# A two-block network on one core: when and behind what the first expert's weights are loaded

## The reference

```python
def first_block(x, ...):
    x = x + _mixer(x, ...)                 # three branches a, b, c; merged @ w_out
    x = x + _expert_choice_ffn(x, ...)

def _expert_choice_ffn(x, norm_g, w_router, w_e_gate, w_e_up, w_e_down):
    xn = _rmsnorm(x, norm_g)
    aff = softmax(xn @ w_router)           # 256 tokens x 16 experts
    gate, idx = top_k(aff transposed, 32)  # each expert takes 32 tokens
    xg = xn[idx]
    h = silu(xg @ w_e_gate[e]) * (xg @ w_e_up[e])     # 1024 -> 1536
    yo = (h @ w_e_down[e]) * gate
    return scatter_add(yo, idx)
```

## Time and profile before

| | us |
|---|---|
| median of three runs | 1536.87 (1536.32 to 1538.96) |
| the profiled execution | 1535.79 |
| its span, first to last instruction | 1534.0 |
| TensorE products busy in the span | 1382.4 (90%) |
| VectorE / ScalarE / GpSimd busy | 523.4 / 480.9 / 197.9 |
| bytes moved | 446.84 MB, mean 291 GB/s |

### The profile page before, as it was taken

One profiled execution on the slowest core, in us unless ns is written; L12 is line 12 of the kernel. 1 busy time (PEld: TensorE's weight loads), 2 busy tenths in 40 slices (PEclk: granted clock), 3 DMA queues, 4 the chain that ended last, 5 costly groups with the idle time before them and its releaser, 6 DMA issues. The chain is left out here.

```text
span 1534.0 us, 18841 instructions
## 1 busy us (share of the span) xinstructions
PE 1382.4 (90%) x7568; PEld 903.0 (59%) x7568; DVE 523.4 (34%) x899; ACT 480.9 (31%) x739; POOL 197.9 (13%) x128
## 2 busy tenths in 40 slices
PE   8999999998777888777788887999999999899998
PEld 7888888543322333223223332878888778788886
DVE  5997877300000000000000001735333526653334
ACT  6766653300000000000000001635444457554443
POOL 0020000000000000000000000352222182122221
PEclk9999999999898888888978889999999999999999
DMA  7664448999999999999999999836565454265640
GB/s 252 195 175 124 119 154 328 418 431 430 429 432 431 432 435 431 431 431 429 432 431 432 434 431 418 325 120 210 174 202 184 157 196 137 92 211 173 202 158 28
DMA packets 117938, 446.84 MB, mean 291 GB/s; under 512 B 8568, under 2 KB 61176, under 8 KB 98816
## 3 DMA queue, kind: packets, MB, share of 16 engines
q1 hardware_dynamic: 117312, 445.47, 75.2%
q10 hardware_dynamic: 576, 0.71, 0.2%
HBM read 445.10 MB, written 1.05 MB: 291 GB/s over the span
## 5 line engine op out<-in xcount | busy, mean ns | idle before, releaser
L1488 PE MATMUL ps<-sb_ring,sb_consts 128*32 128x384 f32 x1760 | 191.5, 593 | 85.7 <-DMA sb_ring<-w_e_up 48.6
L170 PE MATMUL ps<-net_whi,sb_xhi 128*128 128x512 f32 x480 | 189.8, 395 | 1.5 <-DVE sb_xlo L2465 1.0
L1488 PEld LDWEIGHTS ps<-sb_ring,sb_consts 128*32 128x32 f32 x1760 | 61.5, 129 | 215.8 <-issue 106.9
L172 PE MATMUL ps<-net_whi,sb_xlo 128*128 128x512 f32 x480 | 187.1, 390 | 0.0
L171 PE MATMUL ps<-net_wlo,sb_xhi 128*128 128x512 f32 x480 | 187.0, 390 | 0.0
L1510 PE MATMUL ps<-sb_e_ring,sb_hT 128*32 128x512 f32 x540 | 178.4, 646 | 3.3 <-DMA sb_e_ring<-w_e_down 3.3
L1980 ACT ACTIVATE net_whi<-sb_ring 128x2048 fp32r<-128x2048 f32 x64 | 122.2, 1918 | 58.4 <-PE ps L172 55.4
L1583 DVE TENSOR_TENSOR sb_sg<-ps,sb_sg 128x384 f32<-128x384 f32 x16 | 8.9, 557 | 363.7 <-PE ps L1488 363.7
L1993 DVE TENSOR_TENSOR net_wlo<-sb_ring,net_whi 128x2048 fp32r<-128x2048 f32 x46 | 107.1, 2332 | 58.2 <-ACT net_whi L1980 58.2
L1993 POOL TENSOR_TENSOR net_wlo<-sb_ring,net_whi 128x2048 fp32r<-128x2048 f32 x18 | 83.7, 4648 | 215.7 <-ACT net_whi L1980 215.7
L1510 PE MATMUL ps<-sb_mid,sb_hT 128*32 128x512 f32 x180 | 105.9, 751 | 5.3 <-DMA sb_e_ring<-w_e_down 5.3
(11 more groups left out here) (369 smaller groups left out, 2056.0 us busy)
## 6 DMA issues: line engine op xcount, KB each, us to landing
sb_ring<-w_e_gate SPq DMA_DIRECT2D x28, 3072.0 KB, 39.1
sb_e_ring<-w_e_down SPq DMA_DIRECT2D x46, 1536.0 KB, 35.1
sb_ring<-ffn_w_gu SPq DMA_DIRECT2D x88, 512.0 KB, 4.6
sb_ring<-w_e_up SPq DMA_DIRECT2D x14, 3072.0 KB, 39.2
sb_ring<-w_e_up SPq DMA_DIRECT2D x20, 1536.0 KB, 40.8
sb_mid<-w_e_up SPq DMA_DIRECT2D x16, 1536.0 KB, 42.0
sb_mid<-w_e_down SPq DMA_DIRECT2D x15, 1536.0 KB, 32.2
sb_ring<-ffn_w_down SPq DMA_DIRECT2D x22, 1024.0 KB, 4.9
```

The source lines that it names most:

```text
L170: pe.matmul(out, hi, whi, start=start, stop=False)
L172: return pe.matmul(out, lo, whi, start=False, stop=stop)
L1488: mm = pe.matmul(ps[j * CAP:(j + 1) * CAP, GATE if i < 4 else UP, 0:FJ], xgs[:, k, :], rows[:, q * E_FF + j * FJ:q * E_FF + (j + 1) * FJ], ...
```

## The change

Five edits in four places. (1) Units 0 to 3 of expert 0 are issued behind granules 69, 72, 75 and 78 in place of one behind granule 80 and three behind 81; the three waits stand ahead of unit 0 as before. (2) Groups 1 to 3 of expert 0 and the pair of expert 1 move from the experts' SyncE program, behind the barrier, into the mixer's, behind a wait for the mixer's last product. (3) The table's load stays where it is, and is now the first that the experts' program issues. (4) `m.spare` and `m.e_ring` are allocated ahead of the mixer, and the mixer's halves `whi`, `wlo`, `xhi`, `xlo` and `yahi` are given addresses under them, so that both can be named at the same time. (5) `WARM` is 3 in place of 4.

```diff
         st = Stream(ctx, nc, "mix", ring[:, :, :], 5, 5, GRAN)
-        st.place_halves(ctx, nc, "mix")
+        st.hi, st.lo, xhi, xlo = m.mix_whi, m.mix_wlo, m.mix_xhi, m.mix_xlo
...
-        xhi, xlo = sb("xhi", [P, DC, SEQ], F32R), sb("xlo", [P, DC, SEQ], F32R)
...
-        yhi = {"a": sb("yahi", [P, 4, SEQ], F32R), "b": xhi[:, 4:DC, :], "c": chi}
+        yhi = {"a": m.mix_yahi, "b": xhi[:, 4:DC, :], "c": chi}
...
+        EARLY_AT = [n_gran - 13, n_gran - 10, n_gran - 7, n_gran - 4]
...
-                if g == n_gran - 2:
-                    sp.wait_ge(yalo, A_HEADS)
-                    sp.wait_ge(yclo, C_HEADS // 2)
-                    sp.wait_ge(conv_step, 4 * B_TAPS)
-                    load_expert(sp, m, I, 0, 0)
-            for i in range(1, EARLY):
+                if g in EARLY_AT:
+                    if g == EARLY_AT[0]:
+                        sp.wait_ge(yalo, A_HEADS)
+                        sp.wait_ge(yclo, C_HEADS // 2)
+                        sp.wait_ge(conv_step, 4 * B_TAPS)
+                    load_expert(sp, m, I, 0, EARLY_AT.index(g))
+            for i in range(RING, EARLY):
                 if i == RING:
                     sp.wait_ge(yblo, 4)
                 elif i == RING + 1:
...
             load_group(sp, m, I, 0, 0)
-
+            sp.wait_ge(st.used, n_gran)
+            for j in range(1, P // CAP):
+                load_group(sp, m, I, 0, j)
+            load_pair(sp, m, I, 1, 0, True)
...
-WARM = 4
+WARM = 3
...
-            load_group(sp, m, I, 0, 1)
             sp.dma_start(late[:, :], I["c_late"][:, 3 * P:]).then_inc(late_in, 16)
-            for j in range(2, J):
-                load_group(sp, m, I, 0, j)
-            load_pair(sp, m, I, 1, 0, True)
             sp.sem_clear(m.mixer_sems)
...
-                mixer(nc, m, I)
+                with ExitStack() as under:
+                    def below(name, shape, side):
+                        return under.enter_context(nc.sbuf_tensor("mix_" + name, [P, *shape], F32R, side=side))
+
+                    m.mix_whi, m.mix_yahi = below("whi", [5, GRAN], "left"), below("yahi", [4, SEQ], "left")
+                    m.mix_wlo = below("wlo", [5, GRAN], "right")
+                    m.mix_xhi, m.mix_xlo = below("xhi", [DC, SEQ], "right"), below("xlo", [DC, SEQ], "right")
                 m.spare = first.enter_context(nc.sbuf_tensor("sb_spare", [P, SPARES * SLOT], F32))
                 m.e_ring = room("e_ring", (SPARE - RING - RING2 - MID) * SLOT)
+                mixer(nc, m, I)
```

## The result

| | before | after |
|---|---|---|
| median, us | 1536.59 (1536.09 to 1538.96, 4 runs) | 1548.51 (1546.58 to 1549.33, 4 runs) |
| ratio to before | | 1.0069, 95% interval 1.0057 to 1.0081 |
| profiled execution, us (span) | 1535.79 (1534.0) | 1546.58 (1544.8) |

The change made the kernel slower by 0.69% (the quotient of the two medians alone would be 1.0078, inside the interval). 1545.5 was forecast, with a range of 1540.2 to 1548.7: the median lies 3.0 us above the forecast and 0.2 us under the range's upper end. The medians lie 11.9 us apart, the profiled executions 10.8. Where the time went shows in the same views as before. The page first: span, and GB/s by slice.

What follows compares the result with a forecast made beforehand. TensorE was taken to bound the mixer and second block, weight transfers the experts. Late table, slow gather, three units and a landing put the first released load at 314.3 against 305.7: +8.6, so 1545.5 us, range 1540.2 to 1548.7.

Steps and rivals of the forecast that it cites:

- The rule: Experts, bound by weight transfers: they move by as much as the landing at 305.7 us of expert 0's first released load.
- The sum: From the table's landing at 294.05 us to the first released load's landing: 314.3 against 305.7, so +8.6 us.
- What is moved past what: SyncE queue: the table's load keeps its order behind groups and pair, lands at 294.05; the rank copy begins 5.9 us later.
- rival A: Load queue: the table overtakes the pair and isn't held back; 1.85 us faster, 1535.0, no measurable change; chance 10%.
- Terms of the sum: Hand-over to expert 0: table 294.05, copy to gather 0.72, gather 7.4, scaling and start 0.6, three units 5.5, landing 6.05.
- Rival B: Gather: the table is late but the clock holds, gather in 3.7 us; +4.9, 1541.8 us; chance 27%.
- The bound of +2.2: Expert 0's hidden products: at most 2.2 us more if all three units run at the lower clock.
- I cost this at nothing in the mixer: Mixer: gate unit loads among the granules delay nothing; were the cover gone, at most 4 x 3.7 us.
- the loads have cover: Mixer: loads are issued six granules ahead, so a granule landing up to 3.7 us later holds nothing up.
- The idle product, hidden by the wait: Before the turn of the ranks: one product fewer saves 0.9 us, worth nothing while the table is late.
- Rival A's price: Table early: 0.95 us less queueing plus 0.9 us for the idle product, 1.85 us faster, 1535.0.

Runs made afterwards that it cites:

- table-first kernel: The changed kernel with the table's load issued behind group 0, ahead of the wait for the mixer's last product: 1539.27 us, ratio 1.001 to the kernel before.
- new-rooms: The kernel before with only the mixer's halves placed under spare and e_ring; loads, table and four idle products as before: 1540.43 us, ratio 1.0015.
- pause-filled kernels: The changed kernel with nine more idle products between the turn of the ranks and the gather: 1545.59 us, ratio 1.0048 to the kernel before.

## Why the prediction was right, and where it was off

*The rule*, that the experts move by as much as the first refill's landing: shown by the table above to within a microsecond, and with the issue in place of the landing to within half of one. By the landing the profiled executions should lie 10.5 us apart, by the issue 11.2; they lie 10.8 apart. The sum counts 0.95 us as won by a load that finds the queue empty, and the runs don't give that in full.

*What is moved past what*: right. The table landed 0.2 us behind the pair, as forecast, the copy waited for it, and rival A fell. Two runs show it, one that moves only this line forward and one that moves only this line back.

*Terms of the sum.* Group 1 on an empty queue took 6.4 us (forecast 6.05) and the refill 6.3. The bytes at 431 GB/s are 3.65 of either, so the rest is 2.7, above the 2.0 that the Trainium skill (DMA: Bandwidth & Descriptors, the part on the two cost components) gives. Its figure was fitted to transfers issued from GpSimd, and these are issued by SyncE; the measurement decides. Group 1's landing to the pair's took 14.6 (14.8), the gather 7.01 (7.4), start of the hidden products to the third unit 5.44 (5.5). Rival B, the clock that holds, fell with the gather. The errors of these terms, +0.35, +0.25, -0.2, -0.4 and -0.06, cancel, which is luck. The bound of +2.2 for all three units at the lower clock looks too small: of the 5.5 us before, some 2.7 ran at 2.4 GHz, and doubled they make up to +2.7. The forecast doesn't use it.

*The term that was mis-sized* is "I cost this at nothing in the mixer". The last product ended at 274.84, not 272.95; the sum was short by these 1.9 us (316.2 for 314.3), so the forecast of +8.6 stood against 10.8 in the profiled executions. The reason given for the nought, that the loads have cover, was right: between 205 and 275 us neither TensorE nor ScalarE waited for a DMA. What the prediction didn't price was edit 4, the rooms, which I took for a matter of names. Of the 1.9, 0.26 were there at the first product of the mixer (11.12 for 10.86); the other 1.6 are the slower products, as the five traces with the new rooms and a fast start have them (263.6 to 263.7 us for 262.1). Why the place of an operand matters no run shows.

*The idle product, hidden by the wait*: right for the changed kernel. Its 0.9 us as a gain of rival A were too much; without the late table it gave nothing measurable.

*Rival A's price*, 1.85 faster than before, was wrong as well: with the table early the kernel came out at 1.001, not 0.999. The trace puts it down to the slower products and the clock: the last mixer product is 4.15 us later than before, and the gather 2.4 us longer.

*What stays open*: the changed kernel's profiled execution is the fastest of its four; the median lies 1.9 us higher, and with it only 0.2 us inside the range. That the range held for the median owes something to luck. The last section has a candidate, a slow start of the mixer, which no profile of those runs shows.

## What to carry to other kernels

When loads are moved ahead in a queue that keeps its order, look for the small transfer that stays where it was: it now waits for all their bytes, and what hangs on it may be the critical step. Here a preload that ended earlier gained nothing while its rooms were full; what counted was the first moment at which a room came free, and who waited for what up to there. Moving operands to other addresses can have a price (1.6 us of the mixer here): compare the time from product to product.

## What the runs showed of the hardware

The first products of the mixer ran at either of two paces, depending on the run. The table-first kernel's profiled execution began them slowly; the second column is the duration:

```profile
12.06 0.63 PE L172 MATMUL ps<-mix_whi,mix_xlo 128*128 128x512 f32 x1
12.49 0.63 PE L170 MATMUL ps<-mix_whi,mix_xhi 128*128 128x512 f32 x1
...
16.77 0.39 PE L172 MATMUL ps<-mix_whi,mix_xlo 128*128 128x512 f32 x1
17.00 0.40 PE L170 MATMUL ps<-mix_whi,mix_xhi 128*128 128x512 f32 x1
```

The changed kernel's had the fast pace from the start (0.23 us from start to start behind the first product, against 0.43 here). With equal rooms, the last mixer product ended at 277.1 here and at 274.8 there: 2.3 us, nearly all from the start. The new-rooms and the pause-filled kernels show the same slow start. That this is the clock at its lower level, 1.2 GHz, is inferred from the durations: the clock column shows 1.00 over these products, but the trace's first entry for the clock only comes at 27.5 us:

```profile
12.00:16.00 4.00, 4.00 (x11) 3.06 (x10) 4.00 (x7) 4.00 (x8) 0.00 (x0) 1.00 1.11 337
```

The Trainium skill (TensorE: Matmul & The Clock Gate, Part 1) says that the moment of the change isn't tied to a kernel's start and that the same kernel shows different counts of slow products; these traces, of kernels that begin with the same products, agree.

Idle products meant to hold the clock can end later than the work that they cover: where the clock was low ahead of them, they held the turn of the ranks back by 3.3 us. And the clock fell right behind the gather's products of 32 columns, though their weight loads kept the engine filled: in the kernel before, and in the one with the filled pause, where TensorE had paused for 0.17 us only ahead of them (0.50 from 302.5 on, the gather's end at 302.4). In the changed kernel, which began them at 0.50, all 7.01 us of them ran at that level. That their few columns are the reason isn't shown.
